# Prompt attention of a two-layer decoder step: values before the next transposes, low halves before mask and maximum, filler matmuls in equal portions

## The reference

```python
def one_block(args):
    qn, qr, q0 = args
    s = (jnp.einsum('bqhd,bkhd->bhqk', qn, k_nope)
         + jnp.einsum('bqhr,bkr->bhqk', qr, k_rope)).astype(jnp.float32) * SM_SCALE
    q_pos = q0 + jnp.arange(Q_BLOCK)
    s = jnp.where(k_pos[None, :] <= q_pos[:, None], s, -jnp.inf)
    p = jax.nn.softmax(s, axis=-1).astype(v.dtype)
    return jnp.einsum('bhqk,bkhd->bqhd', p, v)
```

```python
q_lat = jnp.einsum('bthd,chd->bthc', q_nope, w_uk)
s_past = (jnp.einsum('bthc,bkc->bhtk', q_lat, past_lat)
          + jnp.einsum('bthr,bkr->bhtk', q_rope, past_rope)).astype(jnp.float32) * SM_SCALE
```

## Time and profile before

| | us |
|---|---|
| median of 3 runs | 2287.74 |
| lowest and highest | 2281.82, 2289.15 |
| the profiled execution | 2287.42 |
| its span | 2285.5 |
| PE busy | 2051.3 (90%) |
| DVE, POOL, ACT busy | 910.4, 755.3, 508.6 |

### The profile page before, as it was taken

The page is one execution under the profiler, slowest core; times in us unless marked ns, Lnnn a source line. Parts: engine busy times, 40 slices in busy tenths (PEclk is TensorE's granted clock), DMA queues, the critical chain, the costliest instruction groups (busy, mean ns, idle before and its releaser), DMA issues.

```text
span 2285.5 us, 33778 instructions
## 1 busy us (share of the span) xinstructions
PE 2051.3 (90%) x12406; PEld 1856.9 (81%) x12406; DVE 910.4 (40%) x1488; ACT 508.6 (22%) x895; POOL 755.3 (33%) x761
## 2 busy tenths in 40 slices
PE   2998898889998999999869988898799999999995
PEld 2997788774398999999869878788626989999994
DVE  7064555552155111421251645555423541133216
ACT  3122444441010100200121234444311110120002
POOL 5332333230034333443253233234200433334434
PEclk9999999998999999999979999999899999999997
DMA  3214011117312221111111231012461122211121
GB/s 113 61 42 148 26 55 60 54 55 235 135 44 64 79 74 55 42 46 51 47 31 45 68 117 57 26 55 66 155 213 54 49 86 65 74 42 47 50 62 76
DMA packets 90956, 167.08 MB, mean 73 GB/s; under 512 B 11641, under 2 KB 36489, under 8 KB 90415
## 3 DMA queue, kind: packets, MB, share of 16 engines
q1 hardware_dynamic: 74244, 135.43, 19.3%
q10 hardware_dynamic: 16572, 29.89, 3.5%
HBM read 141.74 MB, written 24.00 MB: 73 GB/s over the span
## 4 chain that ended last, share of the span: by engine, by line
PE 78%; DVE 11%; issue 5%; ACT 2%; DMA 2%; SPq 1%; ACTq 1%; DVEq 0%; POOL 0%; POOLq 0%
PE PS L525 53%; PE PS L546 6%; PE PS L568 4%; PE PS L616 3%; PE PS L646 2%; PE PS L579 2%; PE PS L603 2%; DVE MX L1239 2%; DVE PTL L1246 2%; PE PS L619 1%; PE PS L671 1%; DVE RT L1167 1%; DMA LATN<-out_lat_s 1%; PE PS L585 1%; DVE PS L1238 1%
## 5 line engine op out<-in xcount | busy, mean ns | idle before, releaser
L444 POOL CAST WH<-RAW 128x512 fp32r<-128x512 f32 (+3 forms) x296 | 192.4, 650 | 1079.4 <-DMA RAW<-in_wstream 1079.4
L446 POOL TENSOR_TENSOR WL<-RAW,WH 128x512 fp32r<-128x512 f32 (+3 forms) x296 | 381.9, 1290 | 23.9
L525 PE MATMUL PS<-XH,WH 128*128 128x344 f32 x1632 | 352.3, 324 | 13.9 <-DVEq L1349 5.5
L525 PE MATMUL PS<-XH,WL 128*128 128x344 f32 x1632 | 349.0, 322 | 0.0
L525 PE MATMUL PS<-XL,WH 128*128 128x344 f32 x1632 | 348.9, 322 | 0.0
L525 PEld LDWEIGHTS PS<-XH,WH 128*128 128x128 f32 x1632 | 275.9, 190 | 18.1 <-DVEq L1349 7.2
L525 PEld LDWEIGHTS PS<-XH,WL 128*128 128x128 f32 x1632 | 276.9, 190 | 0.0
L525 PEld LDWEIGHTS PS<-XL,WH 128*128 128x128 f32 x1632 | 276.3, 190 | 0.0
L467 POOL TENSOR_SCALAR PB<-PB,RC 128x128 f32<-128x128 f32 (+7 forms) x128 | 95.6, 747 | 346.6 <-DVE RC L1233 346.6
L579 PE MATMUL PS<-IDENT,PB 128*128 128x128 f32 x416 | 70.5, 284 | 77.6 <-DVE PTL L1246 77.6
L579 PEld LDWEIGHTS PS<-IDENT,PB 128*128 128x128 f32 x416 | 47.5, 143 | 96.8 <-issue 94.9
(11 more groups left out here) (212 smaller groups left out, 3561.2 us busy)
## 6 DMA issues: line engine op xcount, KB each, us to landing
RAW<-in_wstream SPq DMA_DIRECT2D x232, 256.0 KB, 2.7
PGR<-in_pages SPq DMA_DIRECT2D x96, 320.0 KB, 4.9
PGA<-in_pages SPq DMA_DIRECT2D x32, 320.0 KB, 4.6
spill_g<-FST ACTq DMA_DIRECT2D x48, 172.0 KB, 1.9
SGL<-spill_g ACTq DMA_DIRECT2D x16, 516.0 KB, 4.4
spill_v<-VSTG ACTq DMA_DIRECT2D x16, 512.0 KB, 2.8
VSP<-spill_v SPq DMA_DIRECT2D x8, 1024.0 KB, 5.8
out_y_all<-HT SPq DMA_DIRECT2D x8, 512.0 KB
```

What stands on the lines that cost most here:

```text
L444: pool.tensor_copy(WH[:, slot, 0:size], RAW[:, slot, 0:size]).then_inc(w_high[slot], 1)
L446: pool.tensor_tensor(WL[:, slot, 0:size], RAW[:, slot, 0:size], f(WH[:, slot, 0:size]), ALU.subtract).then_inc(w_split[slot], 1)
L525: last = nc.tensor.matmul(PS[:, 3 * par + c, 0:CH], w[:, slot, at], x(k)[:, c * CH:(c + 1) * CH], start=(k == 0 and n == 0), stop=(k == kt ...
```

## The change

No arithmetic changes. Four things are written in another place:

1. PE: at even n from 2, `values(n/2-1)` stands before `turn(n)`.
2. DVE: the low half of block n-2 stands at the head of step n, before reciprocal, mask, maximum and NB.
3. `fill`: behind the 24 matmuls at the start of a pair, 8 follow each of the steps 0 to 14. Before, steps 0 to 3 and 8 to 11 had 12, steps 4 to 7 had 6, and steps 12 to 15 had none. The evacuations move with them.
4. POOL: the split of the next key weights moves from step 5 to step 9, and those of the two query weights (behind the last pair: of `B_H + 1`) from steps 13 and 15 to behind step 15.

SP's program is the same. Since the last filler matmul now stands behind step 14 instead of step 11, the last slots are released there.

```diff
-        FILL_AT = {-1: (0, 24), 0: (24, 36), 1: (36, 48), 2: (48, 60), 3: (60, 72), 4: (72, 78), 5: (78, 84),
-                   6: (84, 90), 7: (90, 96), 8: (96, 108), 9: (108, 120), 10: (120, 132), 11: (132, 144)}
-        FILL_EVAC = {1: 0, 3: 1, 5: 2, 9: 3, 11: 4, 13: 5}
+        FILL_AT = {-1: (0, 24)} | {n: (24 + 8 * n, 32 + 8 * n) for n in range(15)}
+        FILL_EVAC = {1: 0, 4: 1, 7: 2, 10: 3, 13: 4, 16: 5}
...
-                        if n == 5:
+                        if n == 9:
                             split(l, after)
-                        if n == 13:
-                            split(l, after + 1, only=0)
-                        if n == 15:
-                            if i < PAIRS - 1:
-                                split(l, after + 2)
-                            else:
-                                split(l, after + 1, only=1)
+                    split(l, after + 1)
+                    if i < PAIRS - 1:
+                        split(l, after + 2)
...
                     for n in range(16):
+                        if n >= 2 and n % 2 == 0:
+                            values(r, n // 2 - 1)
                         turn(r, n)
                         if n + 2 < 16:
                             scores(l, i, n + 2)
-                        if n >= 2 and n % 2 == 0:
-                            values(r, n // 2 - 1)
                         fill(l, i, n)
```

More of the change, by code:

```diff
@@ L1230, in _ @@
                     for n in range(18):
-                        if 1 <= n <= 16:
-                            dve.wait_ge(ex_done, 16 * r + n)
-                            v.reciprocal(RC[:, n - 1:n], SUM[:, n - 1:n]).then_inc(rc_done, 1)
-                        if n < 16:
-                            h, j = BLOCKS[n]
-                            row = score_banks(n)
-                            dve.wait_ge(sc_done, 16 * r + n + 1)
-                            own(v.tensor_tensor(row[:, j * P:(j + 1) * P], row[:, j * P:(j + 1) * P], MASK[:], ALU.add))
-                            own(v.tensor_reduce(MX[:, n:n + 1], row[:, 0:(j + 1) * P], AX_X, ALU.max))
-                            v.tensor_scalar(NB[:, n:n + 1], MX[:, n:n + 1], -SCALE, None, ALU.mult).then_inc(mx_done, 1)
                         m = n - 2
```

10 lines of the change are left out of this document (added).

## The result

The changed kernel takes 2341.31 us (median of 4 runs, 2336.73 to 2345.8) against 2286.2 us for the kernel before in the same comparison: a ratio of 1.0243, 95% interval 1.0211 to 1.0274. The profiled execution takes 2337.38 us, its span is 2335.6, so it is 50 us longer than that of before. The direction was predicted, the size was not: 2315, at most 2328.

The account below looks back on a forecast made before the run. The prediction took a loop through TensorE and VectorE as the present bound, replaced by one of VectorE and ScalarE. 2287.4 + 3 (pairs) + 23.4 (seam) + 1 (clock) = 2314.8, said as 2315 us; range 2296 to 2328.

Parts of the forecast that it names:

- eight pairs +3: Eight attention pairs: the new order adds +0.4 us to each, eight times, +3 us.
- seam +23.4: Behind each layer's last pair: the last ring slot is released later, delaying TensorE by +12.5 and +10.9 us, together +23.4.
- clock +1: First matmul behind layer 1's last pair: half clock after the stall, +1.9 us at most, taken as +1.
- moves as a whole: Seam: the time from slot release to TensorE, 21.67 and 19.95 us, stays the same and only shifts later.
- Two signs: Seam: PGA issued within 2 us of block 15's transposes; TensorE waits 10 to 13 us for LATN in both layers.
- +0.4 us a pair: First transposes to key projection: 59.7 to 60.9 us against 60.0 now, middle taken; range -1.5 to +2 a pair.
- loop sum: VectorE and ScalarE's 15 turns in a pair: terms add to 57.5 us, giving a pair of 59.7 to 60.9.
- The 0.9 us estimated for blocks 7 and 8: Normalisation and values stand before the transposes there, lengthening the loop by 0.9 us, from 58.8 to 59.7.
- The filler step: Part 3: the same 144 matmuls fill gaps the loop leaves in any case, so moving them is worth nothing by itself.
- The second loop: Low half, reciprocal, mask, maximum, exponential, high copy, on VectorE and ScalarE without TensorE, sets the pair's length in the new order.
- Rival B: Pair longer by 1 to 2.5 us as TensorE's wait for evacuation pushes scores and maximum: 2320 to 2332, chance 0.13.
- C: Rival: loads not late, or high copy not waiting for the next exponential, so pairs shrink: 2271, chance 0.08.

Follow-up runs that it names:

- e4: Changed kernel with the first sample token's page, UKT, UVF and LATN loads issued ahead of the last weight piece of the ring: 2312.1 us, ratio 1.0101.
- e5: Kernel before with equal filler portions, GpSimd's splits moved, and the sample loads issued ahead of the last ring slots: 2261.7 us, ratio 0.9886.
- e9: Changed kernel with VectorE's reciprocal put back to the head of the step, ahead of the low half: 2307.6 us, ratio 1.0084.
- e2: Kernel before with parts 1 and 2 alone (values ahead of transposes, low half first), filler and splits as before: 2317.6 us, ratio 1.0120.
- e1: Kernel before with parts 3 and 4 alone (equal filler portions, splits moved), TensorE's and VectorE's orders as before: 2296.7 us, ratio 1.0033.
- e13: e11 with the filler's old portions and GpSimd's splits at their old places: 2262.9 us, ratio 0.9884.
- e11: Changed kernel with all three cures, the edits of e4, e8 and e9 (sample loads ahead, side work early, reciprocal first): 2230.2 us, ratio 0.9744.
- e7: Changed kernel with an extra ScalarE copy of 128 x 256 elements ahead of each exponential: 2365.6 us, ratio 1.0348.
- e8: Changed kernel with ScalarE's side work (own_low and the filler's evacuation) put ahead of the exponential: 2301.9 us, ratio 1.0072.
- e6: Kernel before with an extra ScalarE copy of 128 x 256 elements ahead of each exponential: 2291.2 us, ratio 1.0013.
- e14: e11 with TensorE's values of a group behind transposes and scores again: 2250.0 us, ratio 0.9831.

## Why the prediction missed

**The sum.** Predicted: eight pairs +3, seam +23.4, clock +1. The trace has +24.8 for the eight pairs (15.0 + 6.6 + 3.2) and +25.9 for the seam, in which layer 1's longer L757 isn't counted.

**The seam was right.** The gap between the end of the last weight issue and block 15's transposes was put at 2.2 us. With the issue's 0.33 taken off as in the prediction it is 528.75 - 526.55 = 2.20 in layer 0 and 1675.70 - 1673.53 = 2.17 in layer 1. From there to TensorE were to pass 21.67 and 19.95 us; it is 22.49 and 21.54, 0.8 and 1.6 us longer than the "moves as a whole" allowed. In layer 0 that is the issuing of the pages (5.02 us against 4.15); in layer 1 issuing takes 0.6 us of it, and LATN, issued at 1685.33, takes the other 1.0 longer to let TensorE go. Two signs were just off: PGA is issued 3.6 and 3.4 us behind block 15's transposes, not 2, and TensorE waits 13.9 and 12.9 us for LATN, not 10 to 13. e4 and e5 show that the cause is the one named. L757 in layer 1 takes 6.99 us at a granted clock of 0.50, as in layer 0, where it was 5.12 at 0.70: +1.87, where I had taken 1. The Trainium skill (TensorE: Matmul & The Clock Gate, Part 1: The HAM clock gate) has half clock as the default state, and this trace agrees. But the total does not show these 1.87 us: from the start of L757 in layer 1 to the end of the span are 640.65 us before and 640.53 after.

**The step that failed is "+0.4 us a pair".** The eight pairs were put at +3 us and cost +24.8. Two things were wrong in it.

- *The base.* It compares 59.7 to 60.9 us with "60.0 now". Pair 0 of before is a pair in which the values of block 14 ran at half clock; the undisturbed pair is 58.4. One pair was read, and the clock of that stretch was not. Against 58.4 the same loop sum gives +1.3 to +2.5 a pair, and the measured undisturbed pair, 60.9, is the upper end of the sum (its means "replaced by each block's own size"). This alone moves the forecast from +3 to between +10 and +20.
- *Half clock in the loop.* The new waits of 2.15 to 2.4 us before the transposes of blocks 7 and 15 are followed, in most pairs, by stretches at 0.50. The prediction had half clock only at the seam, and put it at nothing in the pairs. In and behind the six pairs it goes with 12.3 us in the changed kernel against 5.7 before, +6.6. It is paid because the chain goes through TensorE at just these places.

The loop itself was right. "That costs nothing where the loop of VectorE and ScalarE is longer, which is everywhere but at blocks 7, 8 and 15" is what the chain of pair 1 shows, though TensorE waits for the normalisation in 62 of the 128 blocks. The 0.9 us estimated for blocks 7 and 8 is 0.80 there, and the 2.6 us from the end of the loop to the key projection are 2.55. What the sum could not show is that the reciprocal's place was a choice: it stands in every turn behind a low half that waits for the high copy, and e9 gets 2.8 us an undisturbed pair by moving it.

**The filler step holds only where it was said.** "Worth nothing by themselves" is about right in the changed kernel's own loop (e2 against e4), which has the idle time to hide them. In the old orders the equal portions are worth 2.5 us a pair (e1), and in the cured ones 33 us (e13 against e11). The reason given (gaps that the loop leaves in any case) takes every block for a gap, but a portion of 12 does lie on TensorE's path in the blocks that had one.

**What held.** The second loop, VectorE and ScalarE without TensorE, exists: the chain shows it between the two places named, e7 and e8 bear out ScalarE's part in it from both sides, and that part was absent before (e6). Rival B's size came nearer (pairs longer by 1 to 2.5 us, 2320 to 2332), though not by its mechanism: the wait of filler for evacuations is 13.3 us in all. C's condition was the high copy no longer held up behind the exponential. No run moves the exponential, so C stays untested; e8 and e11, which move only the side work, come to 2302, and to 2230 with the other two edits, against C's 2271.

## What to carry to other kernels

When an instruction is moved ahead in an in-order queue, its wait moves with it: list what now stands behind that wait and needs none of it. Here that was a reciprocal of 0.15 us, and putting it back ahead gave 36 us. Read the length of a loop from its undisturbed turns, with the granted clock beside them, before a predicted length is compared with it. And a late release of a buffer is paid by all that is queued behind the load which waits for it, so loads that need no slot go ahead of it.

## What the runs showed of the hardware

In this loop half clock was seen behind waits of little over 2 us. The wait of 2.15 us that ends at 251.91 in the changed kernel is followed by a window at 0.66, and the filler matmuls in it take 0.49 us instead of 0.32.

Not every such wait does it. The same transposes in pair 1 stand behind a wait of the same length, and the window behind them is at 1.00:

```profile
332.96 0.66 PE L574 MATMUL PS<-IDENT,PB 128*128 128x128 f32 x4 [2.15 <-POOL PB L466]
```
```profile
333.00:338.00 5.00, 5.00 (x38) 4.76 (x39) 2.55 (x7) 2.09 (x6) 0.37 (x1) 1.00 0.02 3
```

So one execution has three lengths (60.9, 62.1, 63.2 us) for the same work, and what decides between them is open. The kernel before shows the same: all its pairs have a wait of 2.53 us before the transposes of block 14, and four of six are at a mean clock of 0.97, two at 1.00. In e1, e5, e9, e11 and e14 no wait of TensorE inside the six pairs is longer than 1.4 us; all of them are at 1.00 and agree within 0.2 us. So a loop without long waits is not only shorter, its length is also steady.
